# The entrance of the last mixer: tokens' factors put onto the products, twelve channel blocks scaled out of PSUM by VectorE, input tiles in other banks

## The chip, the cores and the metric

The kernel is one launch on one core of a Trainium2 chip. The metric is the device time in microseconds (us); three runs of the kernel before gave 1220.75, 1220.9 and 1222.05 us, median 1220.9 us. Smaller is better. A difference of about 0.2% is what a measurement of this kernel can tell from no change.

## The reference, cut to what matters

Two transformer blocks over 256 tokens of width 1024, in fp32. Before every matrix product stands a norm over the token's channels:

```
def _rmsnorm(x, g):
    y = xf * lax.rsqrt(jnp.mean(xf * xf, axis=-1, keepdims=True) + EPS)
    return (y * g.astype(jnp.float32)).astype(x.dtype)
```

The second block, in which the change lies, begins so:

```
h = h + 0.5 * _swiglu(_rmsnorm(h, ffn1_norm[i]), ffn1_w_in[i], ffn1_w_out[i])
z = _rmsnorm(h, mix_norm[i]) @ w_in[i]
conv_a, conv_gt, q, k, v, r, g_lr = jnp.split(z, SPLIT_POINTS, axis=-1)
y_conv = _conv_module(conv_a, conv_gt, ...)   # a * sigmoid(b), 31-tap causal conv, layer norm
y_gla = _gla(q, k, v, r, g_lr, ...)           # gated linear attention, 4 heads, chunks of 64
h = h + jnp.concatenate([y_conv, y_gla], axis=-1) @ w_out[i]
```

The norm's factor of a token is one number for all channels, so `(x * factor * gain) @ w` equals `factor * ((x * gain) @ w)`: the factor may be put on after the product. In `_gla` the gate is `log_sigmoid(g_lr @ w_gate_up + b_gate)`, summed up along each chunk (`cum`), and all of the attention needs that sum.

## The kernel before, in words

**Weights.** They come as a stream of units of 128 x 3072 numbers, three slots deep. Each unit is split in three pieces of 1024 columns: ScalarE makes the upper part of a piece (`hi`, L1016), VectorE the remainder (`lo`, L1549). A product is three TensorE instructions, L363 to L365 (upper by upper, upper by lower, lower by upper). A unit's slot may be rewritten when the products that read it are done (`s_used`); SyncE starts the load of a unit when the split of the unit three before it is done.

**Tokens.** `x` holds the residual, tokens on partitions. For a product it has to be transposed to `h_hi` and `h_lo`, channels on partitions. There are two ways. The early way (`norm`, L399, `norm_a`, `norm_b`) waits until all of `x` is summed, computes the tokens' factors, and multiplies `x` by a diagonal matrix of these factors, which transposes and scales at once; while it waits, TensorE runs 16 products on zeros (`warm`, L561). It is used for norms 0 and 5, and 8 at the end. The late way (`turn`, L451, `turn_rest`, `late_norm`) transposes the unscaled `x`, two quarters of it amid the last down products of the feed-forward part before and two quarters amid the first products of the next part; the factors are worked out beside that (`late_factors`, L1635) and put on afterwards. Where the output has tokens along the free dimension, the factors are first spread over all partitions by two small products (`spread`, L465) and copied to `rb` by ScalarE. The late way is used for norms 1 to 4, 6 and 7.

**The entrance of the last mixer** (L871 on) uses norm 5, the early way. TensorE then computes four tiles of three channel blocks (units `U_IN2`, `+1`, `+3`, `+4`: a and b of the convolution's gate, then q and k; each 72 products of 256 columns), with unit `U_IN2+2` (a part of r, and g_lr) between the second and the third, and the small gate product (`gate_ready`) after the third. ScalarE moves the twelve blocks from PSUM to `arena`, by Copy or, for the b blocks, Sigmoid (`spots_of`, L1414). The tiles take banks 0, 1 and 2, 3 in turn.

**What follows**, each engine in the order written:
- TensorE: after the fourth tile it waits for `la_done` (L899), then computes the running sums `cum`, 7 convolution taps, the unit `U_IN2+5`, 7 more taps, and then the attention's scores, which wait for `gla_in_done` (L920).
- VectorE: gates the convolution's input (`gated`), and works off 80 taps of the convolution (`conv`, L2108) between splits and steps of the attention. `la_done` comes from L2141, after a chain: the bias is added to the gate product (L2137, `gl_done`); ScalarE takes Abs, Exp and Ln of it (`g_ln_done`), beside 11 taps on VectorE; L2141 puts the two together.
- ScalarE: splits, moves, and the diagonals for TensorE's taps (`tap_diags`).

Of the kernel before, what the change touches and what calls it, by code (L numbers as in the profile page):

```python
# [21 lines left out]
ALU = mybir.AluOpType  # L22
# [3 lines left out]
P = 128  # L26
S = 256
T = S // P
# [105 lines left out]
def build(nc, stream, vectors, masks, x_in, mem_in, pos_in, ple_in, fin_in, out):  # L134
    with ExitStack() as ctx:
# [83 lines left out]
        def q_factor(t, h):  # L219
# [43 lines left out]
        LATE, EARLY = (1, 2, 3, 4, 6, 7), (0, 5, 8)  # L263
# [13 lines left out]

        PE_TAPS = [(3, tap) for tap in range(TAPS)] + [(2, tap) for tap in range(SHARED)]

        PLAIN = [0, 1, 2, 3, 4, 5] + HG_UNITS + [U_MLA, U_MLA + 1, U_MLA + 2, U_UQ, U_UQ + 1, U_UKV] + \  # L280
                list(range(U_IN2, U_IN2 + 7)) + [U_PROJ]
# [75 lines left out]
        def _(pe):  # L357
# [513 lines left out]
            norm(5)  # L871
            for n, u in enumerate(IN2_TILES):
                if n >= 2:
                    pe.wait_ge(s_evac, EV[IN2_TILES[n - 2]])
                for j in range(3):
                    m = cols(u, j, ps[:, (n % 2) * 2 + j // 2, (j % 2) * S:(j % 2) * S + S],
                             5 if n == j == 0 else None)
                m.then_inc(s_used, 1)
                if n == 1:

                    rows(U_IN2 + 2, 0, 256, (4, 5), h_hi, h_lo)
# [34 lines left out]
            pe.wait_ge(s_evac, EV[IN2_TILES[2]])  # L916
            rows(U_IN2 + 5, 0, 384, (0, 1), h_hi, h_lo).then_inc(s_used, 1)
            conv(7, 14)
            pe.wait_ge(s_evac, EV[U_IN2 + 5])
            pe.wait_ge(sem("gla_in_done"), 1)  # L920
            pair_scores(0, kd, qd).then_inc(sem("g_s_ready"), 1)
            pair_scores(6, ku, qu).then_inc(sem("g_s_ready"), 1)
            pe.wait_ge(s_evac, EV[IN2_TILES[3]])
# [88 lines left out]
        def _(act):  # L1012
# [25 lines left out]
            def unit(u, *moves):  # L1038

                split(u + 2)  # L1040
                evac_only(u, *moves)
# [43 lines left out]
            def spread(i):  # L1085
                act.wait_ge(sem("rb_ready"), FFN_NORM.index(i) + 1)
                copy(rb, ps[:, 7, 0:S]).then_inc(sem("rb_done"), 1)
# [294 lines left out]
            for i in range(2, HEADS + 3):  # L1382
# [10 lines left out]
                if i == HEADS + 1:  # L1393
# [18 lines left out]
            spots = [(ga, 0), (gs, 0), (ga, 1), (gs, 1), (ga, 2), (gs, 2), (ga, 3), (gs, 3),  # L1412
                     (gq, 0), (gq, 1), (gk, 0), (gk, 1)]
            def spots_of(n):  # L1414
                def spot(j):
                    dst, i = spots[3 * n + j]
                    return act.activation(dst[:, i, :], ps[:, (n % 2) * 2 + j // 2, (j % 2) * S:(j % 2) * S + S],
                                          ACT.Sigmoid if dst is gs else ACT.Copy)
                return [lambda j=j: spot(j) for j in range(3)]

            unit(U_IN2, *spots_of(0))
            unit(U_IN2 + 1, *spots_of(1))
            unit(U_IN2 + 2,
                 *[lambda t=t: act.activation(gr[:, t, 256:512], ps[:, 4 + t, 0:256], ACT.Silu) for t in range(T)],
                 lambda: copy(glr, ps[:, 6, 0:S]))
            unit(U_IN2 + 3, *spots_of(2))
# [16 lines left out]
            unit(U_IN2 + 4, *spots_of(3))  # L1443
# [8 lines left out]
            unit(U_IN2 + 5, *tok(gv, 0, 384))  # L1452
# [5 lines left out]
            unit(U_IN2 + 6, *tok(gv, 2, P, 384),  # L1458
                 *[lambda t=t: act.activation(gr[:, t, 0:256], ps[:, 2 + t, P:384], ACT.Silu) for t in range(T)])
# [73 lines left out]
        def _(dve):  # L1533
# [107 lines left out]
            def ffn(i):  # L1641
# [62 lines left out]
                dve.wait_ge(sem("rb_done"), i + 1)  # L1704
# [8 lines left out]
                if i == 2:  # L1713
                    residual(4, U0 + CH, range(4), 0.5)
                    lo(None, U0 + CH + 2, 0)
# [382 lines left out]
            norm_a(5)  # L2098
            norm_b(5, "mix2")
# [20 lines left out]
            def gated(i):  # L2120
                return dve.tensor_tensor(glu[:, i, pad:pad + S], ga[:, i, :], gs[:, i, :], ALU.mult)

            split(U_IN2 + 2)
            dve.wait_ge(s_evac, EV[U_IN2])
            gated(0)
            split(U_IN2 + 3)
# [3 lines left out]
            conv(9)  # L2130
            split(U_IN2 + 4)
            conv(19)
# [4 lines left out]
            dve.tensor_tensor(la, ps[:, 7, :].rearrange("p (a b) -> p a b", b=256),  # L2137
                                  V("gb", 0, 256).unsqueeze(1).to_broadcast([P, T, 256]), ALU.add).then_inc(sem("gl_done"), 1)
# [254 lines left out]
```

## Time and profile before

| | |
|---|---|
| runs | 1220.75, 1220.9, 1222.05 us; median 1220.9 us |
| profiled execution | 1219.29 us, of which its span 1217.4 us |
| TensorE busy | 1187.3 us, 98% of the span |
| VectorE, ScalarE busy | 890.0 us (73%), 685.1 us (56%) |
| mean granted TensorE clock | 0.994 |
| chain that ended last | TensorE 91%, VectorE 6%, ScalarE 2% |
| the stage of the change | last down products of the feed-forward part at 862.2 us, first product of the mixer at 871.2 us, `cum` at 915.3 us |

Times of rows count from the start of the span. The rows of the profiled execution are compared with its own 1219.29 us.

### The profile page before, as it was taken

The numbers are of one execution on the slowest core, as the hardware profiler recorded it, in microseconds if no ns is written. First come the engines' busy times: TensorE is split into PE (matmuls) and PEld (weight loads), VectorE is DVE, ScalarE is ACT, GpSimd is POOL, SyncE is SP. The second block draws the span as 40 slices with busy tenths as digits, with TensorE's granted clock in tenths as the row PEclk, the third lists the DMA queues.
The fourth block names the chain that finished last, engine by engine and source line by source line (L and its number), as shares of the span: only waits on it lengthen the run. The fifth ranks groups of instructions, "written<-read, shape, count | busy, mean of one in ns | idle before, by whom it ended". The sixth has DMA issues, their size and how long they took to land.

```text
span 1217.4 us, 21562 instructions
## 1 busy us (share of the span) xinstructions
PE 1187.3 (98%) x8128; PEld 1102.6 (91%) x8128; DVE 890.0 (73%) x1688; ACT 685.1 (56%) x1219; POOL 3.5 (0%) x9
## 2 busy tenths in 40 slices
PE   9999999999999889999999999999999999999996
PEld 7989979999999777999999999999899889999985
DVE  6987878978778667888777766555689676656566
ACT  6854557655557846665555644444557565444454
POOL 0000000000000000000000000000000000000000
PEclk9999999999999989999999999999999999999999
DMA  9544234554545304464545554544444046454540
GB/s 354 210 171 156 105 139 152 211 201 165 202 183 208 129 25 184 166 230 174 205 164 200 201 214 165 198 179 183 172 183 165 13 171 246 169 205 165 199 156 35
DMA packets 21303, 211.48 MB, mean 174 GB/s; under 512 B 2624, under 2 KB 2880, under 8 KB 4480
## 3 DMA queue, kind: packets, MB, share of 16 engines
q1 hardware_dynamic: 20880, 208.90, 46.5%
q0 software_dynamic: 368, 1.84, 0.4%
q8 instruction: 36, 0.59, 0.2%
q14 instruction: 19, 0.16, 0.0%
HBM read 209.68 MB, written 1.05 MB: 173 GB/s over the span
## 4 chain that ended last, share of the span: by engine, by line
PE 91%; DVE 6%; ACT 2%; issue 1%; DMA 0%; SPq 0%; ACTq 0%; DVEq 0%
PE ps L363 27%; PE ps L364 27%; PE ps L365 27%; PE ps L368 7%; PE ps L460 1%; DVE h_lo L1631 1%; DVE w_lo L1549 1%; DVE x L1620 1%; ACT arena L1016 0%; PE ps L782 0%; DMA x<-in_x 0%; PE ps L607 0%; DVE arena L1915 0%; DVE arena L1864 0%; DVE arena L1866 0%
## 5 line engine op out<-in xcount | busy, mean ns | idle before, releaser
L1549 DVE TENSOR_TENSOR w_lo<-raw,w_hi 128x1024 fp32r<-128x1024 f32 (+1 forms) x390 | 448.5, 1168 | 71.9 <-ACT w_hi L1016 71.7
L363 PE MATMUL ps<-h_hi,w_hi 128*128 128x256 f32 x1608 | 455.8, 283 | 0.0
L365 PE MATMUL ps<-h_hi,w_lo 128*128 128x256 f32 x1608 | 455.0, 283 | 0.0
L364 PE MATMUL ps<-h_lo,w_hi 128*128 128x256 f32 x1608 | 455.0, 283 | 0.0
L1016 ACT ACTIVATE w_hi<-raw 128x1024 fp32r<-128x1024 f32 (+1 forms) x390 | 382.8, 1009 | 49.5 <-PE ps L365 46.3
L364 PEld LDWEIGHTS ps<-h_lo,w_hi 128*128 128x128 f32 x1608 | 308.3, 192 | 3.1
L363 PEld LDWEIGHTS ps<-h_hi,w_hi 128*128 128x128 f32 x1608 | 308.3, 192 | 3.1
L365 PEld LDWEIGHTS ps<-h_hi,w_lo 128*128 128x128 f32 x1608 | 308.3, 192 | 0.0
L363 PE MATMUL ps<-w_hi,y_hi 128*128 128x512 f32 (+2 forms) x550 | 211.4, 384 | 2.2 <-issue 1.0
L364 PE MATMUL ps<-w_lo,y_hi 128*128 128x512 f32 (+2 forms) x550 | 208.8, 380 | 0.0
L365 PE MATMUL ps<-w_hi,y_lo 128*128 128x512 f32 (+2 forms) x550 | 207.9, 378 | 0.0
L1651 DVE TENSOR_TENSOR arena<-ps,arena 128x256 f32<-128x256 f32 x176 | 66.4, 419 | 108.8 <-PE ps L365 108.8
L363 PEld LDWEIGHTS ps<-w_hi,y_hi 128*128 128x128 f32 x550 | 103.7, 189 | 20.3 <-issue 3.2
L365 PEld LDWEIGHTS ps<-w_hi,y_lo 128*128 128x128 f32 x550 | 103.4, 188 | 19.2
L364 PEld LDWEIGHTS ps<-w_lo,y_hi 128*128 128x128 f32 x550 | 103.8, 189 | 14.6
L1111 ACT ACTIVATE arena<-arena,vec 128x256 f32<-128x256 f32 x88 | 48.2, 594 | 120.3 <-DVE arena L1651 120.3
L1119 ACT ACTIVATE arena<-arena 128x256 f32<-128x256 f32 x44 | 18.4, 418 | 154.0 <-DVE arena L1651 154.0
L1665 DVE SCALAR_TENSOR_TENSOR arena<-arena,vec 128x254 f32<-128x254 f32 (+1 forms) x176 | 77.2, 481 | 25.4 <-ACT arena L1111 25.1
L363 PE MATMUL ps<-w_hi,h_hi 128*128 128x384 f32 (+3 forms) x208 | 69.4, 334 | 0.0
L365 PE MATMUL ps<-w_hi,h_lo 128*128 128x384 f32 (+3 forms) x208 | 68.4, 329 | 0.0
L364 PE MATMUL ps<-w_lo,h_hi 128*128 128x384 f32 (+3 forms) x208 | 68.4, 329 | 0.0
L368 PE MATMUL ps<-arena 128*128 128x64 f32 (+3 forms) x436 | 62.8, 301 | 2.7 <-DVE arena L1866 1.7
(278 smaller groups left out, 980.9 us busy)
## 6 DMA issues: line engine op xcount, KB each, us to landing
raw<-in_stream SPq DMA_DIRECT2D x129, 1536.0 KB, 6.6
raw<-in_stream SPq DMA_DIRECT2D x3, 512.0 KB, 6.5
x<-in_x SPq DMA_DIRECT2D x2, 512.0 KB, 4.7
arena<-in_mem SPq DMA_DIRECT2D x1, 1024.0 KB, 13.1
x<-in_x POOLq DMA_DIRECT2D x1, 1024.0 KB, 5.3
out<-arena SPq DMA_DIRECT2D x4, 256.0 KB, 2.1
vec<-in_vectors SPq DMA_DIRECT2D x1, 633.0 KB, 8.0
arena<-in_final POOLq DMA_DIRECT2D x1, 512.0 KB, 3.8
```

Source lines behind the costliest of these rows:

```text
L363: pe.matmul(o, lh, rh, start=start, stop=False, skip_group_check=True)
L364: pe.matmul(o, lh, rl, start=False, stop=False, skip_group_check=True)
L365: return pe.matmul(o, ll, rh, start=False, stop=stop, skip_group_check=True)
L368: return pe.matmul(o, l, r, start=start, stop=stop, skip_group_check=True)
L460: m = pe.transpose(ps[:, XT_BANK[k % 4], (k // 4) * S + t * P:(k // 4) * S + (t + 1) * P], x[:, t, k * P:(k + 1) * P], ident)
L1016: return act.activation(o, i, ACT.Copy, scale=scale)
L1111: act.activation(cv[:, g, z * S:(z + 1) * S], tu[:, g, z * S:(z + 1) * S], ACT.Identity, scale=w(4 * z + 2), bias=w(4 * z + 3)).then_inc(s ...
L1119: act.activation(sa[:, g, :], tu[:, g, 0:S], ACT.Silu).then_inc(sem("silu_done"), 1)
L1549: dve.tensor_tensor(w_lo[:, s, a], raw[:, s, a], w_hi[:, s, a], ALU.subtract).then_inc(s_lo, 1)
L1620: dve.scalar_tensor_tensor(x[:, t, r], ps[:, 2 * t + half, :], scale, x[:, t, r], ALU.mult, ALU.add).then_inc(sem("x_done"), 1)
L1651: dve.tensor_tensor(tu[:, g, z * S:(z + 1) * S], ps[:, b, z * S:(z + 1) * S], rb, ALU.mult).then_inc(sem("tu_done"), 1)
L1665: m = dve.scalar_tensor_tensor(c, tu[:, g, z * S:(z + 1) * S - d], w, c, ALU.mult, ALU.add)
```

## The change

Norm 5 goes the late way. On TensorE, two quarters of `x` are turned amid the last down products, two quarters within the first tile, whose products run with the channel slice outside and the three blocks inside; `spread(5)` follows that tile. On ScalarE and VectorE, `late_norm(5)` stands for `norm_a` and `norm_b`, and VectorE computes the factors behind it. The twelve blocks are read from PSUM and multiplied by `rb` on VectorE (`scaled`, three instructions a tile); ScalarE applies Sigmoid in place to the b blocks. Units with tokens on partitions are multiplied by `NORM`, the factors, within ScalarE's moves; the bias of the gate is added by two instructions that also multiply by the factor. Tiles take the bank pairs (4, 2), (3, 1), (0, 2), (3, 1). VectorE's order changes: the 9 and 19 taps become 24 and 4, `scaled(2)` after the 24, `scaled(3)` after the 4 and ahead of the 11.

The core of the diff:

```diff
-            norm(5)
             for n, u in enumerate(IN2_TILES):
-                if n >= 2:
-                    pe.wait_ge(s_evac, EV[IN2_TILES[n - 2]])
-                for j in range(3):
-                    m = cols(u, j, ps[:, (n % 2) * 2 + j // 2, (j % 2) * S:(j % 2) * S + S],
-                             5 if n == j == 0 else None)
+                a, b = TILE_BANKS[n]
+                spots = [ps[:, a, 0:S], ps[:, a, S:2 * S], ps[:, b, 0:S]]
+                if n == 0:
+                    for k in range(KT):
+                        pe.wait_ge(s_lo, pieces(u, (k + 1) * NC3))
+                        if k == 2:
+                            turn_rest(5)
+                        pe.wait_ge(sem("hT_ready"), KT * 5 + k + 1)
+                        for j in range(3):
+                            r = slice(k * NC3 + j * P, k * NC3 + j * P + P)
+
+                            m = three(spots[j], w_hi[:, u % SLOTS, r], w_lo[:, u % SLOTS, r],
+                                      h_hi[:, k, :], h_lo[:, k, :], k == 0 and j != 1, k == KT - 1)
+                else:
+                    if n >= 2:
+                        pe.wait_ge(sem("in2_scaled"), n - 1)
+                    for j in range(3):
+                        m = cols(u, j, spots[j])
                 m.then_inc(s_used, 1)
+                if n == 0:
+                    spread(5)
...
-            norm_a(5)
-            norm_b(5, "mix2")
+            late_norm(5, "mix2", U_FFN2 + CH, 0.5, U_IN2 + 1)
+            late_factors(5)
...
+            def scaled(n):
+
+                dve.wait_ge(s_used, IN2_TILES[n] + 1)
+                a, b = TILE_BANKS[n]
+                for j, src in enumerate((ps[:, a, 0:S], ps[:, a, S:2 * S], ps[:, b, 0:S])):
+                    dst, i = spots[3 * n + j]
+                    m = dve.tensor_tensor(dst[:, i, :], src, rb, ALU.mult)
+                return m.then_inc(sem("in2_scaled"), 1)
+
             split(U_IN2 + 2)
+            dve.wait_ge(sem("rb_done"), SPREAD.index(5) + 1)
+            scaled(0)
+            split(U_IN2 + 3)
             dve.wait_ge(s_evac, EV[U_IN2])
             gated(0)
-            split(U_IN2 + 3)
+            scaled(1)
+            split(U_IN2 + 4)
             dve.wait_ge(s_evac, EV[U_IN2 + 1])
             gated(1)
             link(gated(2))
-            conv(9)
-            split(U_IN2 + 4)
-            conv(19)
+            conv(24)
+            scaled(2)
             split(U_IN2 + 5)
             dve.wait_ge(s_evac, EV[U_IN2 + 3])
             gated(3).then_inc(sem("glu3_ready"), 1)
             dve.wait_ge(sem("gate_ready"), 1)
-            dve.tensor_tensor(la, ps[:, 7, :].rearrange("p (a b) -> p a b", b=256),
-                                  V("gb", 0, 256).unsqueeze(1).to_broadcast([P, T, 256]), ALU.add).then_inc(sem("gl_done"), 1)
+            for t in range(T):
+                m = dve.scalar_tensor_tensor(la[:, t, :], ps[:, 7, t * 256:(t + 1) * 256], NORM[:, t:t + 1],
+                                             V("gb", 0, 256), ALU.mult, ALU.add)
+            m.then_inc(sem("gl_done"), 1)
+            conv(4)
+            scaled(3)
+            dve.wait_ge(sem("in2_scaled"), 4)
             conv(11)
             dve.wait_ge(sem("g_ln_done"), 1)
```

ScalarE's side: after the norm come the splits of `U_IN2+1`, then `spread(5)`, and before each unit's wait the next split; `sigmoids(n, ...)` waits for `in2_scaled` and works in `gs`.

## Rows read from the trace of the kernel before

**Rows 1.** Page, part 1: busy us (share of the span) xinstructions.
```profile
PE 1187.3 (98%) x8128; PEld 1102.6 (91%) x8128; DVE 890.0 (73%) x1688; ACT 685.1 (56%) x1219; POOL 3.5 (0%) x9
```
**Rows 2.** Waits of TensorE, 860 to 962 us: waited for: us, times, longest.
```profile
PE ps L363 <- DVE y_lo L1926: 1.0, 1, 1.0
```
**Rows 3.** Timeline of TensorE around norm 5: start us, us, operation, [idle before].
```profile
862.17 0.39 PE L363 MATMUL ps<-w_hi,y_hi 128*128 128x512 f32 x1
...
863.53 3.65 PE L368 MATMUL ps<-zero 128*128 128x512 bf16 x16
...
871.16 0.36 PE L363 MATMUL ps<-h_hi,w_hi 128*128 128x256 f32 x1
```
**Rows 4.** Timeline of TensorE around norm 4, the late way.
```profile
672.25 1.03 PE L460 MATMUL ps<-vec,x 128*128 128x128 f32 x8
...
674.49 0.28 PE L363 MATMUL ps<-h_hi,w_hi 128*128 128x256 f32 x1
...
676.52 1.10 PE L460 MATMUL ps<-vec,x 128*128 128x128 f32 x8 [0.43 <-DVE h_lo L1631]
677.37 0.36 PE L363 MATMUL ps<-h_hi,w_hi 128*128 128x256 f32 x1
...
681.81 0.69 PE L368 MATMUL ps<-vec,small 128*128 128x128 f32 x4
```
**Rows 5.** Timeline of TensorE, from the fourth tile to the scores.
```profile
906.47 0.47 PE L363 MATMUL ps<-h_hi,w_hi 128*128 128x256 f32 x1
...
915.28 1.05 PE L368 MATMUL ps<-vec,arena 128*128 128x128 f32 x8
916.17 3.19 PE L368 MATMUL ps<-arena 128*128 128x256 f32 x14
...
927.54 5.93 PE L368 MATMUL ps<-arena 128*128 128x256 f32 x46
```
**Rows 6.** Timeline of VectorE, 897 to 932 us.
```profile
897.23 7.62 DVE L2116 SCALAR_TENSOR_TENSOR arena<-arena,vec 128x256 f32<-128x256 f32 x19
904.76 3.49 DVE L1549 TENSOR_TENSOR w_lo<-raw,w_hi 128x1024 fp32r<-128x1024 f32 x3
...
908.71 0.68 DVE L2137 TENSOR_TENSOR arena<-ps,vec 128x512 f32<-128x512 f32 x1
909.31 4.44 DVE L2116 SCALAR_TENSOR_TENSOR arena<-arena,vec 128x256 f32<-128x256 f32 x11
913.98 0.69 DVE L2141 SCALAR_TENSOR_TENSOR arena<-arena 128x512 f32<-128x512 f32 x1 [0.23 <-ACT arena L1433]
...
928.48 2.42 DVE L1549 TENSOR_TENSOR w_lo<-raw,w_hi 128x1024 fp32r<-128x1024 f32 x3
```
**Rows 7.** Timeline of VectorE, 681 to 686 us: last factor, first blocks times `rb`.
```profile
681.08 0.16 DVE L1569 SCALAR_TENSOR_TENSOR small<-small 128x2 f32<-128x2 f32 x1
...
684.56 0.75 DVE L1651 TENSOR_TENSOR arena<-ps,arena 128x256 f32<-128x256 f32 x2
```
**Rows 8.** Timeline of ScalarE, three stretches: a table load, `rb`, a split.
```profile
137.86 1.28 ACT L1261 ACT_TABLE_LOAD   x1
140.86 0.87 ACT L1261 ACTIVATE arena<-ps 128x384 f32<-128x384 f32 x2 [1.72 <-DVE arena L1866]
...
682.53 0.39 ACT L1016 ACTIVATE arena<-ps 128x256 f32<-128x256 f32 x1 [0.69 <-PE ps L368]
...
889.52 2.96 ACT L1016 ACTIVATE w_hi<-raw 128x1024 fp32r<-128x1024 f32 x3
```
**Rows 9.** Windows: us, PE, PEld, DVE, ACT, POOL busy, granted clock, DMA share, GB/s.
```profile
420.80:424.00 3.20, 0.00 (x0) 0.00 (x0) 1.26 (x6) 3.11 (x13) 0.00 (x0) 1.00 0.00 0
424.00:429.00 5.00, 4.95 (x25) 4.36 (x26) 0.29 (x2) 1.37 (x4) 0.00 (x0) 0.66 0.01 3
432.00:436.20 4.20, 0.05 (x1) 0.00 (x0) 3.86 (x17) 0.05 (x1) 0.00 (x0) 0.80 0.00 0
436.20:442.20 6.00, 5.98 (x26) 5.35 (x27) 2.36 (x8) 2.85 (x9) 0.00 (x0) 0.57 0.00 0
```

More of the change, by code:

```diff
@@ L259, in build @@
         FFN_NORM = (1, 3, 4, 6)
[L263 removed]
+        LATE, EARLY = (1, 2, 3, 4, 5, 6, 7), (0, 8)
         LAST = ((0, 0), (1, 0), (0, 1), (1, 1))
@@ L276, in build @@
         IN2_TILES = (U_IN2, U_IN2 + 1, U_IN2 + 3, U_IN2 + 4)
+        TILE_BANKS = ((4, 2), (3, 1), (0, 2), (3, 1))
+        SPREAD = (1, 3, 4, 5, 6)
         PE_TAPS = [(3, tap) for tap in range(TAPS)] + [(2, tap) for tap in range(SHARED)]
         PLAIN = [0, 1, 2, 3, 4, 5] + HG_UNITS + [U_MLA, U_MLA + 1, U_MLA + 2, U_UQ, U_UQ + 1, U_UKV] + \
-                list(range(U_IN2, U_IN2 + 7)) + [U_PROJ]
+                [U_IN2, U_IN2 + 1, U_IN2 + 2, U_IN2 + 3, U_IN2 + 5, U_IN2 + 6, U_PROJ]
         EV = {u: i + 1 for i, u in enumerate(PLAIN)}
@@ L870, in _ @@
             ffn(2)
[L871 removed]
             for n, u in enumerate(IN2_TILES):
[L873 to L877 removed]
+                a, b = TILE_BANKS[n]
[15 more added lines that the diff above has]
+                        m = cols(u, j, spots[j])
                 m.then_inc(s_used, 1)
+                if n == 0:
+                    spread(5)
                 if n == 1:
+                    pe.wait_ge(sem("in2_scaled"), 1)
                     rows(U_IN2 + 2, 0, 256, (4, 5), h_hi, h_lo)
@@ L915, in _ @@
             conv(0, 7)
-            pe.wait_ge(s_evac, EV[IN2_TILES[2]])
-            rows(U_IN2 + 5, 0, 384, (0, 1), h_hi, h_lo).then_inc(s_used, 1)
+            pe.wait_ge(sem("in2_scaled"), 3)
+            rows(U_IN2 + 5, 0, 384, (0, 2), h_hi, h_lo).then_inc(s_used, 1)
             conv(7, 14)
             pe.wait_ge(s_evac, EV[U_IN2 + 5])
+            pe.wait_ge(sem("in2_scaled"), 4)
             pe.wait_ge(sem("gla_in_done"), 1)
@@ L1406, in _, with sigmoids @@
             ffn(2)
-            norm_a(5)
-            norm_b(5, "mix2")
+            late_norm(5, "mix2")
             hi(None, U_IN2 + 1, 1)
             hi(None, U_IN2 + 1, 2)
[L1412 to L1422, printed above, removed]
+            spread(5)
+            def sigmoids(n, *blocks):
+                act.wait_ge(sem("in2_scaled"), n + 1)
+                return [lambda i=i: act.activation(gs[:, i, :], gs[:, i, :], ACT.Sigmoid) for i in blocks]
+            split(U_IN2 + 2)
+            evac_only(U_IN2, *sigmoids(0, 0))
+            split(U_IN2 + 3)
+            evac_only(U_IN2 + 1, *sigmoids(1, 1, 2))
+            act.wait_ge(sem("late_factors"), LATE.index(5) + 1)
             unit(U_IN2 + 2,
-                 *[lambda t=t: act.activation(gr[:, t, 256:512], ps[:, 4 + t, 0:256], ACT.Silu) for t in range(T)],
+                 *[lambda t=t: act.activation(gr[:, t, 256:512], ps[:, 4 + t, 0:256], ACT.Silu, scale=NORM[:, t:t + 1])
+                   for t in range(T)],
                  lambda: copy(glr, ps[:, 6, 0:S]))
-            unit(U_IN2 + 3, *spots_of(2))
+            split(U_IN2 + 5)
+            evac_only(U_IN2 + 3, *sigmoids(2, 3))
             act.wait_ge(sem("gl_done"), 1)
@@ L1442, in _ @@
             tap_diags(0, 7)
-            unit(U_IN2 + 4, *spots_of(3))
+            split(U_IN2 + 6)
             act.wait_ge(sem("cum_ready"), 1)
@@ L1451, in _ @@
             tap_diags(7, 14)
-            unit(U_IN2 + 5, *tok(gv, 0, 384))
+            unit(U_IN2 + 5, *normed(gv, (0, 2), 384))
             tap_diags(14, 21)
@@ L1457, in _ @@
             m.then_inc(sem("gA_low"), 1)
-            unit(U_IN2 + 6, *tok(gv, 2, P, 384),
-                 *[lambda t=t: act.activation(gr[:, t, 0:256], ps[:, 2 + t, P:384], ACT.Silu) for t in range(T)])
+            unit(U_IN2 + 6,
+                 *[lambda t=t: copy(gv[:, t, 384:512], ps[:, 2 + t, 0:P], NORM[:, t:t + 1]) for t in range(T)],
+                 *[lambda t=t: act.activation(gr[:, t, 0:256], ps[:, 2 + t, P:384], ACT.Silu, scale=NORM[:, t:t + 1])
+                   for t in range(T)])
             tap_diags(21, 28)
```

13 lines of the change are left out of this document (5 added, 8 removed).

## The prediction

> **What bounds the kernel now.** I read the page's busy times first. TensorE is busy 98% of the span [rows 1], so a change counts by what it does to TensorE's own queue: its idle time, and its work that isn't product. I next read who TensorE waits for around the change: from 860 to 962 us the longest wait is one of 1.0 us, near the end [rows 2]. So in the whole mixer TensorE sets the pace, and VectorE and ScalarE keep up. The timeline at the entrance shows what this costs: from the last six down products at 862.17 us it is 8.99 us to the first product of the mixer at 871.16 us, and in between stand the 16 products on zeros, 3.65 us of filling [rows 3]. Last I read VectorE's timeline, since the change gives it more to do and TensorE waits for it at one place, `la_done`. There VectorE's last step starts at 913.98 and takes 0.69 us [rows 6], to 914.67 us; TensorE arrives at 915.28 us [rows 5]. The margin is 0.6 us. The change moves both sides of it.
>
> **The entrance.** Norm 4 is the same late way after the same kind of feed-forward part. From its first eight transposes to the first product of the next part (six down products between) it takes 674.49 - 672.25 = 2.24 us. The other eight transposes cost 677.37 - 676.52 = 0.85 us. The four instructions of the spreading take 0.69 us, of which the next product overlaps some 0.25: 0.45 us, an estimate [rows 4]. There was also a wait of 0.43 us ahead of the second eight, because VectorE's `h_lo` came 676.52 - 674.49 = 2.03 us after the first product and only twelve products of 0.12 us covered it [rows 4]. Here 18 products stand there (two slices by three blocks by three), 2.16 us, so I take that wait as gone; if it stayed it would cost up to 0.4. Sum after: 2.24 + 0.85 + 0.45 = 3.54 us, against 8.99 us. **Gain 5.45 us**, bounds 5.0 and 5.7. The factors are ready 681.08 + 0.16 - 676.52 = 4.7 us after the second eight transposes start [rows 4, 7], while the first tile goes on for 0.85 + 54 products of 0.12 = 7.3 us: the spreading waits for nothing. The weights' first piece is split as before, one instruction earlier in VectorE's queue. SyncE's loads hang on splits, which all come earlier or within a microsecond of before, and each has a tile's time to land: nothing.
>
> **Middle.** From the second tile to the end of the fourth TensorE's work is the same, so all moves by -5.45 us, if the new waits (`in2_scaled`) cost nothing. I follow VectorE and ScalarE. The first tile ends at about 862.17 + 2.24 + 0.85 + 8.75 = 874.0 us (a tile is 915.28 - 906.47 = 8.81 at the most [rows 5]). ScalarE's `rb` copy starts 682.53 - 681.81 = 0.72 us behind the start of the spreading [rows 4, 8]: 874.7. The splits of `U_IN2+2` are queued behind it, on ScalarE 2.96 us for three [rows 8], on VectorE 3.49 [rows 6], a microsecond behind: VectorE ends at 879.5. `scaled` is three operations like L1651, two of which take 0.75 us [rows 7]: 1.05 us for three. So 880.55; TensorE wants it, for banks of `U_IN2+2`, at 883: hidden. Then in turn: a sigmoid (0.4), first piece of `U_IN2+3`, VectorE's split 882.0 to 885.5, gate and `scaled(1)` 886.9, two sigmoids and a first piece 888.55, split 892.0, two gates 892.8, 24 taps of 0.4 (19 in 7.62 [rows 6]) 902.3, `scaled(2)` 903.35, split 906.8, gate 907.15, two gate biases of 0.4 in place of one of 0.6 to 907.95, 4 taps 909.5. TensorE needs each of these later than it comes. The units' moves with a factor are ScalarE's same instructions with a scale: nothing. On ScalarE twelve moves become four sigmoids: it gains, but it sits off the path.
>
> **The new wait.** The fourth tile ends at 915.28 - 5.45 = 909.83 us. TensorE then waits for `la_done`, and behind the waiting instruction in its queue stands all the rest of the mixer. `la_done` now stands behind `scaled(3)`, which waits for that very tile. After the tile, VectorE must do: see the semaphore (0.2, an estimate: a product's 0.28 less its 0.12 spacing, and a little), `scaled(3)` 1.05, its own wait 0.1 (estimate, 0 to 0.2), 11 taps 4.36 (4.44 with the last one's tail), the last step 0.69 [rows 6], start of TensorE 0.05. Sum 6.45 us; bounds 6.1 and 7.0. ScalarE's three functions don't end last: they ran from 909.39 (908.71 + 0.68) to about 913.9, 4.5 us [rows 6], and now from 907.95 to 912.5, before the taps end at 915.5. So `cum` starts at 909.83 + 6.45 = 916.28 us, against 915.28: **+1.0 us**. The entrance's gain is given back here, whatever VectorE does ahead of it.
>
> Further on: `gla_in_done` came by 928.48 on VectorE [rows 6], TensorE needed it at 927.54 + 2.9 = 930.4 (7 taps, as 14 instructions in 916.17's row take about 2.9) [rows 5]. VectorE's last step is 915.6 - 913.98 = 1.6 us later and so is `gla_in_done`, 930.1; TensorE is at least 1.0 us later, 931.4. No wait. Behind that VectorE waits for TensorE, so the rest moves with TensorE.
>
> **The clock.** The trace has two idle stretches of TensorE over 3 us. The first lies in 420.80 to 424.00, and in the five microseconds behind it the granted clock is 0.66: (1 - 0.66) x 5 / 0.5 = 3.4 us at the lower of its two levels, 1.2 GHz. The second is 432.00 to 436.20, and the six microseconds behind it show 0.57, so 5.2 us at 1.2 GHz [rows 9]. Work at half the rate loses half of that time: 1.7 and 2.6 us. The new idle stretch is 6.2 us, longer than both, so I expect the fall; the products behind it, `cum` and the taps, fill TensorE without pause. I take **+2.1 us**, the middle; bounds 0 (no fall) and 3.4 (the second's 0.80 in its idle part is another 1.7 us at the lower level; all 6.8 us behind the restart would lose 3.4).
>
> The Trainium skill, "TensorE: Matmul & The Clock Gate", section "HAM oscillation — how this bites in real kernels", speaks against this change: an engine that sits idle waiting is throttled, and the work after the wait runs at half rate; it prices that at half of the throttled time, which is how the rows above were priced. A plain count of idle time would give +1.0 us, the page's way +3.1; the trace shows the fall at both places. The same skill, "VectorE: DVE Perf Modes", section "The TRN2 errata — SBUF-src ops pay a fixed extra latency per instruction", has VectorE at 120 + n cycles of 0.96 GHz for a PSUM operand, 0.39 us for 256 columns, a little dearer than ScalarE's; three would be 1.18 us, and the sum by that 0.1 us more. The row (0.75 for two) decides.
>
> **Sum.** -5.45 + 6.45 + 2.1 = +3.1 us. The profiled execution: 1219.29 + 3.1 = 1222.4 us. The median of the runs shown stands 1.6 us above that execution, so 1220.9 + 3.1 = 1224.0 us, with +2.0 to +4.4 as this case's own range.
>
> **Rivals.**
> - *The clock holds.* TensorE waits the 6.2 us but is granted full speed behind it. Then +1.0 us: 1221.9. For it: each stretch has its own phase, and the first fall in the trace touched only 3.4 us. Against: both stretches that could show it lost the clock. Chance 0.17.
> - *VectorE is late on top.* My schedule has VectorE free at 909.5 and the tile's semaphore at 910.0, only 0.5 us. It hands to ScalarE and back four times before. If each loses 0.4, or if the table load for Sigmoid (1.28 us [rows 8]) stood behind the wait, `la_done` comes 1 to 2 us later: about +4.4, 1225.3. Against the latter: at 137.86 the load ran before its activation's wait, which ended only at 140.86 [rows 8]. Chance 0.17.
> - *The gain survives.* If `cum` needn't wait, TensorE keeps 5.45: 1215.4. The mechanism decides where the work between tile and `la_done` is under 5.45 us. For it: it takes only 1 us less than the rows give, so a 6.45 that overlaps more than in the row before, with no fall of the clock, would be no change or a slight gain, at best 1219.9. Against: the steps are a chain in one queue, 11 taps of which alone take 4.36. Chance 0.06 for anything faster by over 0.2%, none of it near 1215.4 unless I misread the order.
> - The forecast itself: 0.60.
>
> **How the numbers follow.** About 0.2% (2.4 us) is what can be told from no change: 1218.5 to 1223.3 counts as the same. Slower: 0.85 of the forecast's 0.60 and all 0.17 of a late VectorE, 0.68. Faster 0.06. Same: the clock that holds (0.17) and the forecast's low end (0.09), 0.26. The range takes in a clock that costs half a microsecond and a VectorE that is 2 us late: 1221.3 to 1226.4.
>
> **What would show it.** Right: transposes (L460's line) amid the last down products; 3.5 us in place of 9.0 at the entrance; the fourth tile ends near 910 us; then TensorE idle for 6.2 us, waiting for VectorE's last gate step, with 11 taps right before that; `cum` near 916.3; granted clock near 0.6 in the five microseconds behind it. Wrong: a wait at any `in2_scaled`; the fourth tile later than 910.5; `cum` before 915.3; or a clock of 1.00 at 917 to 921.

## The result, and the profile after

The changed kernel takes 1223.99 us (median of 20 executions, 1221.42 to 1226.07), the kernel before, in 20 executions beside it, 1220.86 us. The ratio is 1.0024, with a 95% interval of 1.0018 to 1.0031: the change makes the kernel 3.1 us slower. It takes 5.5 us out of the entrance, and one wait of 6.3 us further on, with a slower clock behind it, gives back more than that.

The page of the changed kernel, part 1, as in [rows 1]:
```profile
PE 1186.7 (97%) x8100; PEld 1103.3 (90%) x8100; DVE 893.5 (73%) x1699; ACT 683.8 (56%) x1212; POOL 3.5 (0%) x9
```
TensorE has 28 products less: 16 on zeros and the 32 with the diagonal matrix are gone, 16 transposing ones and four of the spreading are new. VectorE has eleven instructions more. No share moved enough to tell a story, so the reader has to go to the stretch itself.

The two profiled executions can't be laid over each other by their clocks. In the one of after (span 1222.2 us, against 1217.4) the point where the last six down products are next comes at 864.43 us, against 862.17 [rows 3]. (In the kernel before these six products start there; in the changed kernel the first eight transposes start there and the six follow. "Behind the down products" below means from this point.) All of these 2.26 us arise ahead of the change: the first eight transposes of norm 4 start at 674.51 us in after, against 672.25 [rows 4]. The 34 products on zeros at the very start take 10.48 us in after and 9.24 us in before, but only 0.52 us of that is left at 72 us. The timelines of TensorE there, before and after, show the same products behind the same wait:
```profile
72.38 2.89 PE L368 MATMUL ps<-arena 128*128 128x64 f32 x24 [1.72 <-DVE arena L1866]
...
72.90 3.28 PE L372 MATMUL ps<-arena 128*128 128x64 f32 x24 [1.72 <-DVE arena L1883]
```
Eleven microseconds later the difference is 2.13 us (83.48 against 85.61). The windows, before and after, show what came in between, on code that the change doesn't touch:
```profile
72.00:100.00 28.00, 27.62 (x185) 27.63 (x186) 24.57 (x39) 14.91 (x24) 0.00 (x0) 1.00 0.33 120
...
72.00:100.00 28.00, 27.10 (x173) 27.10 (x174) 23.29 (x36) 12.80 (x22) 0.00 (x0) 0.94 0.27 98
```
One execution kept the full clock there and the other did not. So I count from the last six down products from here on: what happened behind them is free of this offset. (With it the spans differ by 4.8 us; without it 2.6 us are left.)

The timeline of TensorE after, from the entrance to the mixer's last products (start us, us, operation, idle before):
```profile
864.43 1.03 PE L464 MATMUL ps<-vec,x 128*128 128x128 f32 x8
...
866.68 0.28 PE L367 MATMUL ps<-h_hi,w_hi 128*128 128x256 f32 x1
...
868.84 1.04 PE L464 MATMUL ps<-vec,x 128*128 128x128 f32 x8
869.63 0.36 PE L367 MATMUL ps<-h_hi,w_hi 128*128 128x256 f32 x1
...
876.19 0.60 PE L372 MATMUL ps<-vec,small 128*128 128x128 f32 x4
876.55 0.36 PE L367 MATMUL ps<-h_hi,w_hi 128*128 128x256 f32 x1
...
911.91 0.28 PE L369 MATMUL ps<-h_hi,w_lo 128*128 128x256 f32 x1
...
918.46 2.07 PE L372 MATMUL ps<-vec,arena 128*128 128x128 f32 x8 [6.26 <-DVE arena L2178]
...
966.63 0.50 PE L367 MATMUL ps<-w_hi,y_hi 128*128 128x512 f32 x1 [1.01 <-DVE y_lo L1943]
```
The entrance is now the two sets of transposes amid products (2.25 and 0.79 us) and a spreading that costs 0.36 us: 3.40 us in place of 8.99 [rows 3]. The last product of the fourth tile starts at 911.91 us. Then TensorE stands idle for 6.26 us, and `cum` starts at 918.46 us, 54.03 us behind the down products, where it was 915.28 - 862.17 = 53.11 us [rows 5]. The eight products of `cum` themselves take 2.07 us in place of 1.05 [rows 5]: they run at half rate.

The waits of TensorE after, same stretch (waited for: us, times, longest); [rows 2] has only the second:
```profile
PE ps L372 <- DVE arena L2178: 6.3, 1, 6.3
PE ps L367 <- DVE y_lo L1943: 1.0, 1, 1.0
```
The timeline of VectorE after says what the 6.26 us are made of:
```profile
909.78 1.66 DVE L2133 SCALAR_TENSOR_TENSOR arena<-arena,vec 128x256 f32<-128x256 f32 x4
...
912.23 1.09 DVE L2149 TENSOR_TENSOR arena<-ps,arena 128x256 f32<-128x256 f32 x3 [0.79 <-PE ps L369]
913.35 4.44 DVE L2133 SCALAR_TENSOR_TENSOR arena<-arena,vec 128x256 f32<-128x256 f32 x11
917.71 0.69 DVE L2178 SCALAR_TENSOR_TENSOR arena<-arena 128x512 f32<-128x512 f32 x1
```
VectorE is done with its four taps early enough to wait 0.79 us for the fourth tile itself. It isn't busy when the tile lands. All that TensorE waits for comes behind the tile in VectorE's queue: three scalings, eleven taps, and the one step that `la_done` needs. In [rows 6] the same eleven taps and the same step ran while TensorE still worked on the tile.

Windows after: the idle stretch and what follows (columns as in [rows 9]):
```profile
912.10:918.40 6.30, 0.09 (x1) 0.00 (x0) 6.13 (x16) 6.27 (x13) 0.00 (x0) 0.72 0.31 129
918.40:923.40 5.00, 4.95 (x19) 4.47 (x20) 5.00 (x13) 3.70 (x5) 0.00 (x0) 0.67 0.01 2
923.40:928.00 4.60, 4.60 (x27) 4.52 (x26) 4.60 (x6) 4.04 (x11) 0.00 (x0) 1.00 0.00 0
```
The granted clock is 0.67 in the five microseconds behind the restart, so (1 - 0.67) x 5 / 0.5 = 3.3 us at 1.2 GHz, and 1.65 us lost; then it is 1.00 again. In the kernel before, the same place was work without a gap:
```profile
915.20:920.20 5.00, 5.00 (x31) 4.62 (x30) 4.66 (x13) 4.98 (x11) 0.00 (x0) 1.00 0.00 0
```
A second way gives the same number. From `cum` to the mixer's last products it is 46.52 us before (99.63 us behind the down products, less 53.11) and 966.63 - 918.46 = 48.17 us after, with the same products and the same wait of 1.0 us in it: 1.65 us more. I use this difference below as the price of the clock, since it catches all of the loss, in one number per kernel.

### The profile page after: what moved, and what is told of

Its sections match the earlier page's. It is cut to its first block, busy times and chain, and to the rows that moved or that the text cites. A ratio compares the mean times of both kernels' runs of the same rounds, so it can differ in the third digit from the quotient of the medians.

```text
span 1222.2 us, 21520 instructions
## 1 busy us (share of the span) xinstructions
PE 1186.7 (97%) x8100; PEld 1103.3 (90%) x8100; DVE 893.5 (73%) x1699; ACT 683.8 (56%) x1212; POOL 3.5 (0%) x9
## 3 DMA queue, kind: packets, MB, share of 16 engines
HBM read 209.68 MB, written 1.05 MB: 172 GB/s over the span
## 4 chain that ended last, share of the span: by engine, by line
PE 92%; DVE 5%; ACT 2%; issue 1%; POOL 0%; ACTq 0%; DVEq 0%; POOLq 0%
PE ps L367 27%; PE ps L368 27%; PE ps L369 27%; PE ps L372 8%; PE ps L464 1%; DVE h_lo L1651 1%; DVE w_lo L1569 1%; DVE x L1640 0%; ACT arena L1034 0%; PE ps L786 0%; DVE arena L2133 0%; PE ps L611 0%; DVE arena L1932 0%; DVE arena L1881 0%; DVE arena L1883 0%
```

## The experiments

Two theories of the wait. *The queue:* `scaled(3)` waits for the fourth tile, so everything between it and `la_done` in VectorE's queue starts only when the tile has landed, and the wait is the length of that list, whatever VectorE does ahead of it. *The work:* VectorE has more to do since the change (twelve scalings and more), runs late, and TensorE waits for the sum. By the first the order decides, by the second the amount. Beside them stands the question whether the clock's fall costs what the forecast said. Edits are against the changed kernel. All of them but the last do the same arithmetic on VectorE as the changed kernel. The edits are shown in short words: `split`, `gated`, `conv` and `scaled` stand with the semaphore waits that belong to them, "gate bias" for the two instructions that add it, "last gate step" for the instruction at L2178.

**The last gate step first.** The gate's bias goes right behind `scaled(2)`, the last gate step ahead of `scaled(3)`, and thirteen taps go behind the scores, into `conv(19)`. Nothing is left out of VectorE's work.
```
 scaled(2)
+gate bias -> gl_done
 split(U_IN2 + 5); gated(3)
-gate bias -> gl_done
-conv(4); scaled(3); conv(11)
+conv(2)
 last gate step -> la_done
-conv(13)
+conv(2); scaled(3); conv(11)
...
-conv(6)
+conv(19)
```


> The kernel after, with VectorE's order changed: the gate bias right behind scaled(2), then the split and gate 3, 2 taps, the last gate step, and only then the fourth tile's scaling; 13 of the taps that stood ahead of the scores' inputs go into the later pause before the second mask. Queue theory (the entrance's 5.5 us are real and are given back because the last gate step stands in VectorE's queue behind scaled(3), which waits for the fourth tile, and 11 taps; the clock adds 1.6 to 2.6): the last gate step ends 0.6 us before the fourth tile does, TensorE waits under 0.5 us there, the clock stays at 1.00, and what is left is the entrance's gain less up to 1 us where the moved taps overfill the pause: -5.5 to -4.5 us against the kernel before, ratio 0.9955 to 0.9963. Work theory (the twelve scalings are 4 us more on VectorE, which now bounds the mixer by its sum, in whatever order): the wait only moves, and the time stays within 1.5 us of the kernel after, ratio 1.001 to 1.004.

Measured: 1215.44 us against 1221.49, ratio 0.9949 [0.9935, 0.9964]. The waits of TensorE, 855 to 970 us, have one line left:
```profile
PE ps L367 <- DVE y_lo L1943: 1.0, 1, 1.0
```
Timeline of TensorE:
```profile
911.88 1.05 PE L372 MATMUL ps<-vec,arena 128*128 128x128 f32 x8
```
Timeline of VectorE (bias, last gate step, scalings, the moved taps):
```profile
905.10 0.86 DVE L2167 SCALAR_TENSOR_TENSOR arena<-ps,small,vec 128x256 f32<-128x256 f32 x2
...
910.55 0.69 DVE L2175 SCALAR_TENSOR_TENSOR arena<-arena 128x512 f32<-128x512 f32 x1
...
912.08 1.09 DVE L2149 TENSOR_TENSOR arena<-ps,arena 128x256 f32<-128x256 f32 x3
...
936.04 7.60 DVE L2133 SCALAR_TENSOR_TENSOR arena<-arena,vec 128x256 f32<-128x256 f32 x19
```
Window behind the tile:
```profile
911.80:916.80 5.00, 5.00 (x31) 4.62 (x30) 4.92 (x14) 4.98 (x8) 0.00 (x0) 1.00 0.59 243
```
The step now ends at 911.24 us, ahead of the tile's end, and `cum` follows the tile at once, 911.88 - 864.27 = 47.61 us behind the down products: 5.50 us earlier than before. From there to the last products it is 46.52 us, the time before, and the clock stays at 1.00. The whole gain of the entrance arrives, and the theory of the work falls: VectorE does the same work, and TensorE waits for none of it but the 1.0 us at the mixer's end that the kernel before has too. This version beats both kernels. The ratio is a little lower than I had expected (0.9955 to 0.9963), and the interval takes that in. The same kernel once more, on another chip:

> The kernel of e1 (gate bias and last gate step early, 13 taps in the later pause) once more, for a tighter interval and beside e10. Queue theory: -5.5 us against before (its trace showed 94.1 us from the first transposes to the output products against 99.6), ratio 0.9950 to 0.9960. If e1's -6 us was partly chance of its few runs, it comes out nearer to -5.5.

Measured: 1216.21 us against 1221.45, ratio 0.9949 [0.9936, 0.9962]; `cum` to the last products 46.51 us. One execution of 2249 us is left out of the comparison.

**Zeros in the wait.** TensorE gets 24 products on zeros ahead of its wait, which change no output. The wait stays, the idleness doesn't.
```
+pe.wait_ge(sem("gl_done"), 1)
+warm(24)
 pe.wait_ge(sem("la_done"), 1)
```


> The kernel after, with 24 products on zeros (0.23 us each, 5.5 us) put into TensorE's wait for the last gate step. Queue theory with the clock as its second term: the running sums start at the same place behind the fourth tile (6.4 us), but the granted clock is 1.00 through the wait and behind it, so the running sums and 7 taps take 3.7 us and not 5.4: 1.6 to 2.1 us less than the kernel after, +1.0 to +1.5 us against before, ratio 1.0008 to 1.0013. Rival (the clock is no price, the third microsecond comes from elsewhere, the start of the run or the load on VectorE): as the kernel after, 1.0024.

Measured: 1222.06 us, 1.0002 [0.9993, 1.0011], for an expected 1.0008 to 1.0013 that the interval still reaches. Timeline of TensorE:
```profile
920.02 1.16 PE L372 MATMUL ps<-vec,arena 128*128 128x128 f32 x8 [1.02 <-DVE arena L2180]
```
Windows, up to `cum` and behind it:
```profile
913.30:920.00 6.70, 5.63 (x27) 2.52 (x27) 6.17 (x16) 6.66 (x14) 0.00 (x0) 1.00 0.35 145
920.00:925.00 5.00, 4.98 (x28) 4.60 (x29) 5.00 (x13) 3.90 (x5) 0.00 (x0) 1.00 0.00 2
```
`cum` starts 54.03 us behind the down products, as in the changed kernel, to the hundredth. The clock stays at 1.00, and `cum` to the last products is 46.61 us, 0.09 over before. The mean granted clocks of whole executions say the same without a profile: 0.986 to 0.990 in all 20 of the changed kernel (median 0.989), 0.990 to 0.993 in the twelve with zeros in the wait (median 0.992). So the two costs come apart: the place of `cum` is VectorE's list, and of the 1.65 us behind it all but 0.09 are the clock. What is left in this kernel, +1.0 us at the place, is what a forecast that only counts idle time would have given.

**The scalings behind the step.** `scaled(3)` goes behind the last gate step, and the eleven taps stay ahead of it, so they no longer wait for the tile.
```
 conv(4)
-scaled(3)
 conv(11)
 last gate step -> la_done
+scaled(3)
 conv(13)
```


> The kernel after, with scaled(3) moved behind the last gate step, nothing else. Queue theory: VectorE no longer stands 0.8 us idle for the fourth tile nor scales 1.1 us ahead of the step, so the last gate step ends 15 taps after the gate bias, 4.4 us behind the fourth tile in place of 6.4; TensorE waits 4.2 us, the clock still falls (a wait of 4.2 us lost it in the kernel before), and the total is 2.0 us less than after: +1.1 us against before, ratio 1.0009. Work theory: the same work in another order, as after, 1.0024.

Measured: 1222.19 us, 1.0007 [0.9998, 1.0015]. Timeline of TensorE:
```profile
914.76 2.08 PE L372 MATMUL ps<-vec,arena 128*128 128x128 f32 x8 [4.27 <-DVE arena L2176]
```
Window behind it:
```profile
914.70:919.70 5.00, 4.93 (x16) 4.31 (x17) 4.96 (x14) 4.97 (x7) 0.00 (x0) 0.50 0.00 2
```
The wait is 4.27 us, 2.0 less: 1.1 for the scalings and 0.79 for VectorE's own wait at the tile, both of which left the path. `cum` comes 52.03 us behind the down products, 1.1 us earlier than before. But the clock takes 2.5 us (49.01 us from `cum` on, window 0.50), more than behind the longer wait. Here the list starts when VectorE is free and not with the tile; the wait is the part of it that reaches past the tile.

**The taps behind the step.** The eleven taps go behind the last gate step.
```
 scaled(3)
-conv(11)
 last gate step -> la_done
-conv(13)
+conv(24)
```


> The kernel after, with the 11 taps moved from ahead of the last gate step to behind it; scaled(3) stays ahead. Queue theory: the step now waits for ScalarE's Ln (2.4 us behind the fourth tile) and not for scaled(3) (1.3 us behind it), and ends 3.1 us behind the tile; TensorE waits 3.0 us in place of 6.3, the total is 3.3 us less than after and up to 0.8 less again if the clock keeps up longer; VectorE loses 1 us waiting, which the later pause takes: -0.2 to -1.0 us against before, ratio 0.9992 to 0.9999. Work theory: VectorE's lost microsecond makes it 1 us worse than after, 1.0032.

Measured: 1222.82 us, 1.0009 [0.9999, 1.0019]. I had expected 0.9992 to 0.9999, and this missed. The waits of TensorE tell why:
```profile
PE ps L372 <- DVE arena L2177: 3.1, 1, 3.1
PE ps L372 <- DVE arena L2196: 2.4, 1, 2.4
```
Windows, behind the first wait, in the second, and behind that:
```profile
914.40:919.40 5.00, 4.91 (x28) 4.54 (x29) 5.00 (x14) 4.98 (x10) 0.00 (x0) 1.00 0.00 0
...
929.60:932.40 2.80, 0.42 (x2) 0.03 (x2) 2.77 (x12) 2.62 (x9) 0.00 (x0) 1.00 0.97 382
932.40:937.40 5.00, 4.99 (x34) 4.78 (x35) 5.00 (x11) 2.65 (x4) 0.00 (x0) 0.59 0.52 168
```
Timeline of VectorE, the last gate step:
```profile
913.74 0.69 DVE L2177 SCALAR_TENSOR_TENSOR arena<-arena 128x512 f32<-128x512 f32 x1 [1.20 <-ACT arena L1451]
```
The first wait shrinks from 6.3 to 3.1 us, though less than by the taps' 4.4: the step now waits 1.20 us for ScalarE's logarithm, which the taps had covered. And the taps, 4.4 us of them, stand ahead of `gla_in_done` as they did ahead of `la_done`, so a second wait of 2.4 us arises at the scores. The list was moved from one semaphore to the next. The clock holds behind the first wait and falls behind the second: of the 5.63 us that this stretch takes over before, 2.40 are the second wait and 3.2 the clock. The profiled execution (1223.96 us) is the longest of the eleven and has the lowest mean clock of them, 0.988 against 0.989 to 0.991. By its trace the kernel would be 3.4 us over before, and the interval ends at 2.3. So the other executions lost less to the clock than this one.

**The taps past the scores.** To see whether that explanation is the right one, the same eleven taps go past `gla_in_done` too.
```
 scaled(3)
-conv(11)
 last gate step -> la_done
...
-conv(6)
+conv(17)
```


> The kernel of e4 (the last gate step ahead of the 11 taps, scaled(3) ahead of it), with these 11 taps moved on into the pause before the second mask. e4 showed a second wait of 2.4 us for the scores' inputs, which also lost the clock. Queue theory: every piece of VectorE's queue ahead of a step that TensorE waits for costs in full, so without the taps the second wait is gone; the first stays at 3.1 us. Sum: -5.5 + 3.3 (wait and start) = -2.2 us, plus a clock loss of 0 to 2.5 for a wait of 3.1 us: -2.2 to +0.3 us against before, ratio 0.9982 to 1.0002, and at the place no wait at the scores. Rival (VectorE has too much to do in the mixer, a wait removed at one place comes back at the next): e4's 1.0009 or more, the second wait now at the masks.

Measured: 1220.97 us against 1221.45, 0.9996 [0.9987, 1.0006] (one execution of 2358 us left out). Of the two waits one is left:
```profile
PE ps L372 <- DVE arena L2177: 3.1, 1, 3.1
```
Window behind it:
```profile
914.00:919.00 5.00, 3.65 (x14) 3.36 (x15) 4.39 (x11) 5.00 (x11) 0.00 (x0) 0.66 0.05 20
```
The second wait is gone, while `cum` stays at 50.84 us as in the kernel before this one, so it was the place of the taps that made the second wait. But this time the clock falls at the wait of 3.1 us, only in its last 0.3 us (granted clock 0.95 over the wait), and takes 1.56 us (48.08 us from `cum` on).

**The changed kernel once more**, beside three others on one chip:

> The kernel after as it stands, run beside the three others so that they have it on the same chip. Both theories: +2.5 to +3.5 us against before, ratio 1.002 to 1.003; at the place, the running sums 54.0 us behind the first transposes, then 1.7 to 2.6 us lost to the clock.

Measured: 1224.18 us against 1221.40, 1.0023 [1.0013, 1.0033]. `cum` at 54.02 us, idle 6.26 us, 48.10 us from there on: the first profile repeats within 0.1 us.

**The bias earlier, the taps left.** Of the first experiment only the bias's move. ScalarE gets its input earlier; the list behind the tile stays.
```
 scaled(2)
+gate bias -> gl_done
 split(U_IN2 + 5); gated(3)
-gate bias -> gl_done
```


> The kernel after, with the gate bias moved ahead of the split of U_IN2+5 and gate 3 (3.8 us earlier), the last gate step left where it is. Queue theory: ScalarE's three functions end 3.8 us earlier, but they weren't what the step waited for; the fourth tile, its scaling and 11 taps still are. As after, within 0.2 us at the place. Rival (the chain over ScalarE is what holds the step): 3 us less than after, 1.0000 against before.

Measured: 1225.26 us, 1.0026 [1.0017, 1.0036]. ScalarE's last function before the step moves from 49.35 us behind the down products (913.78 - 864.43) to 45.61 (907.96 - 862.35):
```profile
907.96 0.63 ACT L1451 ACTIVATE arena<-arena 128x512 f32<-128x512 f32 x1
```
The wait of TensorE doesn't move:
```profile
PE ps L372 <- DVE arena L2178: 6.3, 1, 6.3
```
Windows behind it:
```profile
916.30:921.30 5.00, 4.93 (x16) 4.31 (x17) 5.00 (x14) 2.79 (x4) 0.00 (x0) 0.50 0.01 2
921.30:926.30 5.00, 5.00 (x25) 4.62 (x24) 4.96 (x7) 4.45 (x11) 0.00 (x0) 0.87 0.00 0
```
`cum` is at 54.02 us as in the changed kernel, so ScalarE isn't the end of the chain there. The clock's price is 3.13 us, almost twice that of the changed kernel, behind the same 6.3 us.

**Four taps more in the list.** The sum of VectorE's work is the same; four taps move from ahead of `scaled(3)` to behind it.
```
-conv(4)
 scaled(3)
-conv(11)
+conv(15)
```


> The kernel after, with the 4 taps that stand ahead of scaled(3) moved behind it, so 15 and not 11 stand between the fourth tile and the last gate step. VectorE does the same work. Queue theory: each tap there is paid in full, 4 x 0.396 = 1.6 us more than after, TensorE's wait 7.9 us in place of 6.3: ratio to before 1.0037 to 1.0042 (the clock as after). Work theory: the same amount before the step, so the same time less VectorE's longer idle time: +0 to +0.3 us against after.

Measured: 1225.89 us, 1.0032 [1.0021, 1.0043]; the expected 1.0037 to 1.0042 lies in the interval. The wait of TensorE:
```profile
PE ps L372 <- DVE arena L2177: 7.8, 1, 7.8
```
Timeline of VectorE:
```profile
913.63 6.03 DVE L2133 SCALAR_TENSOR_TENSOR arena<-arena,vec 128x256 f32<-128x256 f32 x15
```
Fifteen taps take 6.03 us where eleven took 4.44, and `cum` moves from 54.03 to 55.61 us: 1.58 us for 1.59. Each instruction in the list counts in full, and VectorE's longer idleness ahead of the tile counts for nothing.

**Zeros at the entrance.** Everything from the second tile on is pushed back, by 24 products on zeros and their wait behind the spreading. If VectorE's work set the place of `cum`, this slack would be taken up in the wait.
```
 spread(5)
+pe.wait_ge(sem("rb_done"), SPREAD.index(5) + 1)
+warm(24)
```


> The kernel after, with 24 products on zeros (5.5 us) put behind the first tile's spreading: the entrance's gain is given away before the middle, and VectorE gets 5.5 us more for it. Queue theory: the wait for the last gate step is bound to the end of the fourth tile, so it stays 6.2 to 6.3 us, all is 5.5 to 6 us later than after: +8.6 to +9.2 us against before, ratio 1.0070 to 1.0076. Rival (VectorE can't keep the pace of the earlier tiles; the last gate step comes at VectorE's own time): the wait shrinks to 1 us or so and the total is that of after, 1.0024.

Measured: 1229.85 us, 1.0065 [1.0051, 1.0079]; the expected 1.0070 to 1.0076 lies in the interval. The waits of TensorE:
```profile
PE ps L372 <- DVE arena L2180: 6.3, 1, 6.3
PE ps L372 <- ACT arena L1036: 0.5, 1, 0.5
```
`cum` is at 59.90 us, 5.9 later, and the wait is still 6.3 us. VectorE had 5.9 us more to get ahead, and got nothing from it. By the theory of the work it should have shrunk.

**The order alone, without the change.** The kernel before gets the early gate step of the first experiment: the bias ahead of the split, the last gate step after two more taps. The other nine taps of its list go behind the step, but stay ahead of the scores (the diff is against the kernel before).
```
 split(U_IN2 + 4)
-conv(19)
+conv(24)
+gate bias -> gl_done
 split(U_IN2 + 5); gated(3)
-gate bias -> gl_done
-conv(11)
+conv(2)
 last gate step -> la_done
-conv(13)
+conv(17)
```


> The kernel before, entrance and all, with only VectorE's order changed as in e1: the gate bias behind 24 taps and ahead of the split, the last gate step after 2 further taps, 17 taps behind it. Queue theory: in the kernel before TensorE waited for none of these steps (its margin was 0.6 us), so an earlier last gate step brings nothing: within 0.2 us at the place, ratio 0.9995 to 1.0005. Rival (the order is what makes e1 fast, not the entrance): 0.995 to 0.998.

Measured: 1221.9 us against 1221.45, 1.0002 [0.9993, 1.0011]. `cum` at 53.12 us, 46.51 us from there on, both as before. An early gate step isn't worth anything by itself. Between the changed kernel and the first experiment it is worth 5.50 + 2.57 = 8.1 us at the place, or by the ratios (1.0024 - 0.9949) x 1221 = 9.2 us (the second ratio alone is uncertain by 1.8 us), because there a wait stands in its way that the kernel before doesn't have.

`cum` and the clock over all kernels, in us (place: start of `cum` behind the last six down products; granted: mean granted clock over the 10 us from `cum` on; clock: `cum` to the last products, less 46.52; where a second wait lies in it, that is in the number):

| kernel | wait | place | granted | clock | ratio |
|---|---|---|---|---|---|
| before | none | 53.11 | 1.00 | 0 | 1 |
| order alone | none | 53.12 | 1.00 | 0.0 | 1.0002 |
| after | 6.3 | 54.03 | 0.84 | 1.65 | 1.0024 |
| after, again | 6.3 | 54.02 | 0.85 | 1.58 | 1.0023 |
| gate first, twice | none | 47.61, 47.60 | 1.00 | 0.0 | 0.9949 |
| zeros in the wait | 1.0 | 54.03 | 1.00 | 0.09 | 1.0002 |
| scalings behind | 4.3 | 52.03 | 0.75 | 2.49 | 1.0007 |
| taps behind | 3.1 and 2.4 | 50.84 | 1.00, then 0.66 | 5.63 (with the second wait) | 1.0009 |
| past the scores | 3.1 | 50.84 | 0.85 | 1.56 | 0.9996 |
| bias early | 6.3 | 54.02 | 0.69 | 3.13 | 1.0026 |
| four more | 7.8 | 55.61 | 0.73 | 2.69 | 1.0032 |
| zeros first | 6.3 | 59.90 | 0.80 | 2.03 | 1.0065 |

The loss that the two ends of the stretch give and the granted clock agree in every row with a single wait: 10 us times (1 - granted), the half of the time at the lower level, is the clock's column to 0.1 us. Place and clock together agree with the ratio within its interval in every row but "taps behind".

## Why the prediction was right

On the clock of the kernel before, the times of the changed kernel are 2.26 us less than its profile's.

- **The entrance, -5.45 us.** The parts were 2.24, 0.85 and 0.45; they measured 2.25, 0.79 and 0.36. The wait ahead of the second transposes, 0.43 us in [rows 4], is gone, as 18 products of 0.12 us should do it. The fourth tile was to end at 909.83 us; its last product ends at 911.91 + 0.12 - 2.26 = 909.77. The first experiment shows the gain arriving at the end: 5.50 us.
- **VectorE's margin, 0.5 us.** VectorE had to be free before the tile, or the list would start late. It was idle 0.79 us. The schedule was 0.3 us too careful, which cost the forecast nothing, and no `in2_scaled` held TensorE up.
- **The new wait, 6.45 us.** From 909.77 to `cum` at 918.46 - 2.26 = 916.20 it is 6.43 us. The scalings were 1.09 for 1.05, the taps 4.36 up to the last step (917.71 - 913.35), the step 0.69 and the start 0.06. `cum` is 0.92 us later than before, for +1.0. That this is the list and not ScalarE or VectorE's load is shown by the bias (no change), by four taps more (+1.58) and by the zeros at the entrance (no change of the wait).
- **No wait at the scores.** Right. The forecast margin was 1.3 us. In the trace VectorE's last input ends at 931.88 us and TensorE is through its seven taps at about 932.37 + 3.0 = 935.4, some 3.5 us later; 1.65 us of the difference is the clock's loss, which holds TensorE back too. In the kernel with the taps behind the step, TensorE came to the scores 2.4 us ahead of their inputs.
- **The clock, +2.1 us.** Here it was 1.65 us, in the repeat 1.58. This is the term furthest off, by 0.45 us. Over the seven profiles with a single wait of 3 us or more it was 1.6 to 3.1 us, and behind the first wait of the kernel with the taps behind the step it was nothing. So the bounds of 0 and 3.4 were about as wide as they had to be. That it is the clock is shown by the zeros in the wait, which give it back at the same place of `cum`. The rival in which it holds doesn't hold for this kernel. The Trainium skill, "TensorE: Matmul & The Clock Gate", section "HAM oscillation — how this bites in real kernels", prices the time at the lower clock at half of it. The trace agrees: 0.67 over 5 us is 3.3 us at the lower level, and 1.65 us were lost.
- **The sum.** +3.1 us was forecast. At the place the trace has +0.92 + 1.65 = +2.57 us, the medians have 3.1 us with an interval of 2.2 to 3.8. The half microsecond between forecast and place is the clock's term, and the medians can't tell it from nothing. That forecast and median agree to a tenth is luck. The profiled execution was forecast at 1222.4 us and took 1224.02; the 2.26 us that arose ahead of the change are in that.
- **The rivals.** The table load ran ahead of the wait for the scaling, as in [rows 8]: on ScalarE after, the load is done while the activation that needs it still waits for VectorE.
```profile
880.07 1.28 ACT L1432 ACT_TABLE_LOAD   x1
...
882.79 0.42 ACT L1432 ACTIVATE arena<-arena 128x256 f32<-128x256 f32 x1 [1.44 <-DVE arena L2149]
...
902.78 1.28 ACT L1432 ACT_TABLE_LOAD   x1 [4.73 <-PE ps L369]
905.37 0.42 ACT L1432 ACTIVATE arena<-arena 128x256 f32<-128x256 f32 x1 [1.30 <-DVE arena L2149]
```
(At the third tile, the lower pair, the load itself comes behind a wait of 4.73 us for TensorE's tile, and only the activation waits for the scaling.) VectorE wasn't late on top. The surviving gain had a chance of 0.06 for this kernel and didn't come; the first experiment shows that it took only a change of order.

What the prediction didn't say is that the wait was avoidable. Its sentence that the gain is given back "whatever VectorE does ahead of it" was right, and pointed at the remedy: the step must leave the list, not the work leave VectorE.

## What to carry to other kernels

In an in-order queue, an instruction that others wait for is as late as the last thing that stands ahead of it, whether it needs that or not. When a change puts a new wait into a queue, list everything between it and the next semaphore that another engine waits for, and count that list in full from the awaited event; then move the awaited step ahead of the wait, and move other work past every such semaphore and not only the first. A gap in TensorE costs its length and, behind it, what the clock takes: here 1.6 to 3.1 us in seven profiles with one gap of 3.1 us or more, nothing behind one of 3.1. If the gap can't go, products on zeros in it save the second part, as they did in the one kernel that tried it (1.56 of 1.65 us). One profile shows the clock's price for one execution only; look at the mean clock of the others before trusting it.

## What the runs showed of the hardware

- Gaps of one length did not cost the same. Behind a wait of 6.3 us the clock took 1.65, 1.58, 3.13 and 2.03 us in four profiles of three kernels; behind one of 4.3 us it took 2.5 us. What decides is how long the lower level outlasts the wait, not how long the wait is. TensorE in the 10 us from `cum` on, changed kernel and bias early:
```profile
918.46:928.46 10.00, 10.00 (x48) 9.44 (x49) 9.96 (x19) 8.14 (x15) 0.00 (x0) 0.84 0.00 1
...
916.37:926.37 10.00, 10.00 (x39) 8.99 (x40) 9.96 (x19) 7.30 (x14) 0.00 (x0) 0.69 0.00 1
```
  That is 3.2 and 6.2 us at the lower level, and half of it was lost. Why it lasts so much longer in one of them is not shown.
- The price isn't a property of the kernel alone. The same 24 products behind the same wait of 1.72 us kept the full clock in the profile of the kernel before and not in that of the changed one (1.00 and 0.94 over 28 us), and no line of the diff lies in that stage. The executions of the changed kernel have mean clocks from 0.986 to 0.990. That its two profiles agree within 0.1 us is therefore no proof that a third would.
- A wait of 3.1 us left the clock at 1.00 in one kernel and brought it to 0.66 in the next, at the same place; in the second the fall came in the last 0.3 us of the wait. In the first of them the following wait of 2.4 us brought it to 0.59. Up to that first wait the two kernels are the same; they differ only in the taps that VectorE does behind the step. With one profile of each, the difference may be one between executions. This stays open.
- The first 34 products on zeros took 9.24 us in one profiled execution and 10.48 us in another, of the same products; 0.52 us of the 1.24 was left at 72 us, as a wait of 0.47 us behind them took up part of it. Before two traces are compared, count from a mark just before the change.
- One execution each of two kernels took 2249 and 2358 us, nearly twice the usual. Nothing that the runs show says why.
